# Streaming fp32 weights in five slots that hold the raw chunk and its low half in one place, instead of two raw and four split slots

## The chip, the core and the metric

The kernel runs on one core of one Trainium2 chip. Times are device microseconds of that core, for one launch. Before the change the median of three runs is 1150.75 us (1149.22 to 1153.69). A core has TensorE (PE, the matrix engine), VectorE (DVE), ScalarE (ACT), GpSimd (POOL) and SyncE (SP, which here only issues transfers), and 16 DMA engines that move data between HBM and SBUF. Each compute engine works through its own list of instructions in order and waits on semaphores for the others.

## What is computed

A trunk of two layers over 256 positions of width 1024, all in float32. Cut to what matters here:

```python
for i in range(DEPTH):                        # DEPTH = 2
    h = rmsnorm(x, norm_mix[i])
    q, k, v, cglu, sc_b, sc_c, sc_h, gates = split(h @ w_in[i])
    y_a = window_attention(q, k, v, attn_sinks[i], bias) @ w_attn_out[i]
    c = causal_dwconv(ca * sigmoid(cb), conv_dw[i]) + conv_dw_bias[i]   # 31 taps
    y_b = silu(layernorm(c, ...)) @ w_conv_out[i]
    y_c = (sc_b * causal_dwconv(sc_c * sc_h, sc_conv[i])) @ w_sc_out[i]
    mix = g[0] * y_a + g[1] * y_b + g[2] * y_c                          # g = sigmoid(gates)
    x = x + mix @ w_mix_out[i]
    h2 = rmsnorm(x, norm_ffn[i])
    x = x + (silu(h2 @ w_ffn_gate[i]) * (h2 @ w_ffn_up[i])) @ w_ffn_down[i]
    x = x + (p[i] @ w_ple[i]) * sigmoid(rmsnorm(x, norm_ple[i]) @ w_ple_gate[i])
return rmsnorm(x, norm_final)
```

Each large product is made of three: value and weight are both split into a high half (rounded to the type fp32r) and a low half (what the rounding left), and hi·hi, lo·hi and hi·lo are added in PSUM.

## The kernel before, in words

**Weights.** All weights of both layers are one stream of 184 chunks (92 a layer) of 1 MB, each 16 blocks of 128 by 128, in the order in which TensorE uses them. SP loads a chunk as it is (`w_raw`), ACT rounds it (`w_hi`, function `round_chunk`, operations on line 660), DVE subtracts (`w_lo = w_raw - w_hi`, function `low_chunk`, line 1021). `w_hi` and `w_lo` have four slots each (`RING`), `w_raw` has two (`RAW_RING`). A chunk of strips is 48 matmuls of 256 columns, one of the token-wise products (branches, FFN up and gate) 24 matmuls of 512 columns.

**What lets a chunk in.** SP's loop waits, before the load of chunk n, for `lo_ready` of chunk n-2: DVE has subtracted it and its raw slot is free (line 329, 330). ACT rounds chunk n = c + 4 in the place in its program that `after_chunk(c)` marks, and there also waits for `strip_done` to pass `AFTER[c]`, that is, until TensorE has finished chunk c = n-4, whose slot is overwritten. DVE subtracts at the same mark in its own program.

**What stands around it.** The rounding and the subtraction are placed by hand between the other work of ACT and DVE: gates, softmax, the convolution's taps on DVE (`taps`, line 1145), the products that ACT makes for POOL's convolution adds (`conv_products`, ring of four, POOL line 1476). So an engine that waits for a chunk holds up whatever its program has next. Three such places are spoken of below. In the first, `norm` of the first layer: ACT rounds chunk 2 before `root` (line 688), DVE subtracts chunk 2 before the reciprocal (line 1030) that all of `h` depends on. In the second, DVE's `branch_product` of `conv_out` (lines 1274, 1278) stands behind the subtraction of chunk 48 (140 in the second layer), and TensorE's `turn_mix` (line 546) waits for it. In the third, ACT's first FFN gate (line 948) and DVE's first FFN product (line 1365) stand behind chunk 58 (150), and TensorE's `turn_ffn` (line 582) waits for that product.

TensorE works through the chunks with `strip`, `tok_group`, `strips_late` and `strip_quad`, waits for `lo_ready` once a chunk, and adds to `strip_done` at the end of each strip. At the start SP issues x, chunk 0 in two halves, chunk 1 and the parameters (`prms`), then enters the loop. POOL transfers the relative bias: a spread of 2.5 MB at 14 us and the load of 1.5 MB of it at 58 us.

Of the kernel before, what the change touches and what calls it, by code (L numbers as in the profile page):

```python
# [25 lines left out]
P = 128  # L26
D_MODEL = 1024
SEQ = 256
DEPTH = 2
# [23 lines left out]
BPC = 16  # L53
RING = 4
RAW_RING = 2
BANKS = 4
# [13 lines left out]
STRIPS, CHUNKS = _s, _b // BPC  # L70
assert CHUNKS % RING == 0 and STRIPS % BANKS == 0
USES = STRIPS // BANKS
# [49 lines left out]
def build(nc, x, p, wstream, prm, gain, sink_rows, table, onehot, ident, out):  # L122
    ctx = ExitStack()
    with ctx:
        def sb(name, shape, dt=F32):
            return ctx.enter_context(nc.sbuf_tensor(name, shape, dt))
# [6 lines left out]

        w_raw = sb("w_raw", [P, RAW_RING, BPC * P])
        w_hi = sb("w_hi", [P, RING, BPC * P], F32R)
        w_lo = sb("w_lo", [P, RING, BPC * P], F32R)

# [72 lines left out]

        raw_loaded = [sem(f"raw_loaded{i}") for i in range(RAW_RING)]
        half_loaded = sem("half_loaded")
# [98 lines left out]
        def f32(ap):  # L311
            return ap.bitcast(F32)

        block = ctx.enter_context(nc.Block())


        @block.sync
        def _(sp):
            for k in range(2):
                sp.dma_start(xs[:, k * DT // 2:(k + 1) * DT // 2, :], x[:, k * DT // 2:(k + 1) * DT // 2, :]).then_inc(x_in[k], 16)  # L320
            half = BPC * P // 2
            sp.dma_start(w_raw[:, 0, 0:half], wstream[0][:, 0:half]).then_inc(half_loaded, 16)
            sp.dma_start(w_raw[:, 0, half:], wstream[0][:, half:]).then_inc(raw_loaded[0], 16)
            sp.dma_start(w_raw[:, 1, :], wstream[1]).then_inc(raw_loaded[1], 16)
            sp.dma_start(prms[:, :, :], prm).then_inc(prm_in, 16)

            with sp.Fori(1, DEPTH * CHUNKS // RAW_RING) as i:
                for j in range(RAW_RING):
                    sp.wait_ge(lo_ready, i * RAW_RING + j - RAW_RING + 1)
                    sp.dma_start(w_raw[:, j, :], wstream[i * RAW_RING + j]).then_inc(raw_loaded[j], 16)  # L330
            for b in range(TB):
                for h in range(2):
                    sp.wait_ge(out_dve if h else out_act, b + 1)
                    sp.dma_start(out[b, :, h * 512:(h + 1) * 512], y[:, b, h, :]).then_inc(out_stored, 16)
            sp.wait_ge(out_stored, 4 * 16)
# [3 lines left out]
        def _(pe):  # L339
            def mm3(bank, blk, hi, lo, first, last):  # L340

                slot, col = blk // BPC % RING, blk % BPC * P
                o = psum[bank][:, 0:SEQ]
                wh, wl = w_hi[:, slot, col:col + P], w_lo[:, slot, col:col + P]
                nc.tensor.matmul(o, wh, hi, start=first, stop=False, skip_group_check=True)  # L345
                nc.tensor.matmul(o, wh, lo, start=False, stop=False, skip_group_check=True)  # L346
                return nc.tensor.matmul(o, wl, hi, start=False, stop=last, skip_group_check=True)  # L347

            def strip(L, s, blk, src, ktiles, ds=0, dc=0, ready=None, amid=None, half=False):
# [5 lines left out]
                for k in range(ktiles):  # L355
                    if half and k == 0:
                        pe.wait_ge(half_low, 1)
                    elif (blk + k) % BPC == 0 or k == 0:
                        pe.wait_ge(lo_ready, L * CHUNKS + dc + (blk + k) // BPC + 1)
                    if ready is not None:  # L360
                        ready(k)
                    if amid is not None and k == AMID:
                        amid()
                    mm = mm3(bank, blk + k, hi[:, t0 + k, :], lo[:, t0 + k, :], k == 0, k == ktiles - 1)
                mm.then_inc(strip_done, 1)

            def strip_quad(L, s, blk, n):

                for k in range(DT):
                    for part in range(2):  # L370

                        pe.wait_ge(hlo_ready if part else hhi_ready, (L * 2 + n // 2) * DT + k + 1)
                        for e in range(4):
# [4 lines left out]
                            o = psum[(s + e) % BANKS][:, 0:SEQ]  # L378
                            slot, col = (blk + e * DT) // BPC % RING, (blk + e * DT + k) % BPC * P
                            wh, wl = w_hi[:, slot, col:col + P], w_lo[:, slot, col:col + P]  # L380
# [9 lines left out]
            def tok_group(L, s, c, src, bank, use, ready=None, amid=None, mid=None):  # L390

                hi, lo, t0 = src
                for half in range(2):
                    slot = (c + half) % RING
                    pe.wait_ge(lo_ready, L * CHUNKS + c + half + 1)
# [20 lines left out]
            def strips_late(L, s, blk, src, ktiles, n, early, ready, amid, amid_at):  # L416
# [3 lines left out]
                for part in (range(early), range(early, ktiles)):  # L420
                    for e in range(n):
# [5 lines left out]
                        for k in part:  # L427
# [4 lines left out]
                            if e == 0:  # L432
                                ready(k)
                            mm = mm3(bank, g, hi[:, t0 + k, :], lo[:, t0 + k, :], k == 0, k == ktiles - 1)
                        if part.stop == ktiles:
# [216 lines left out]
        def _(act):  # L652
# [8 lines left out]

            def round_chunk(L, n, after=None, dc=0, dn=0):

                act.wait_ge(raw_loaded[n % RAW_RING],
                            (L * (CHUNKS // RAW_RING) + dn // RAW_RING + n // RAW_RING + 1) * 16 if isinstance(dn, int)
                            else (L * (CHUNKS // RAW_RING) + dn + n // RAW_RING + 1) * 16)
                if after is not None:
                    act.wait_ge(strip_done, L * STRIPS + after)
                copy(w_hi[:, n % RING, :], w_raw[:, n % RAW_RING, :]).then_inc(hi_ready, 1)

# [47 lines left out]
            for L in range(DEPTH):  # L718
                def after_chunk(c, i=0):

                    if c + RING >= CHUNKS:
                        if L < DEPTH - 1:
                            round_chunk(L, c + RING, AFTER[c])
                    elif isinstance(i, int):
                        round_chunk(L, c + RING, AFTER[c])
                    else:
                        round_chunk(L, c + RING, 2 * RING * i + AFTER[c], dn=(RING // RAW_RING) * i)

# [37 lines left out]
                round_h(L * 3)  # L766
                round_chunk(L, RING - 1)
                for t in range(DT):
# [237 lines left out]
        def _(dve):  # L1006
# [8 lines left out]

            def low_chunk(L, n, after=None, dn=0):

                dve.wait_ge(hi_ready, L * CHUNKS + dn + n + 1)
                if after is not None:
                    dve.wait_ge(strip_done, L * STRIPS + after)  # L1020
                nc.vector.tensor_tensor(w_lo[:, n % RING, :], w_raw[:, n % RAW_RING, :], f32(w_hi[:, n % RING, :]),  # L1021
                                        ALU.subtract).then_inc(lo_ready, 1)
# [60 lines left out]
            for L in range(DEPTH):  # L1083
# [21 lines left out]
                raw_gate(1, 2)  # L1105
                low_chunk(L, RING - 1)
                raw_product(cv[:, 1, CPAD:], 1, 3, 1)

                def after_chunk(c, i=0):
                    if c + RING >= CHUNKS:  # L1110
                        if L < DEPTH - 1:
                            low_chunk(L, c + RING, AFTER[c])
                    elif isinstance(i, int):
                        low_chunk(L, c + RING, AFTER[c])
                    else:
                        low_chunk(L, c + RING, 2 * RING * i + AFTER[c], dn=RING * i)

# [505 lines left out]
```

## Time and profile before

| | |
|---|---|
| median of 3 runs | 1150.75 us |
| the profiled execution, its own time | 1149.08 us |
| its span, first to last instruction | 1147.3 us |
| TensorE busy | 1112.1 us (97%) |
| VectorE busy | 811.9 us (71%) |
| ScalarE busy | 697.5 us (61%) |
| GpSimd busy | 414.4 us (36%) |
| weight chunks loaded | 183 whole of 1024 KB, 2 halves of 512 KB |
| HBM read | 199.19 MB, 177 GB/s over the span |

The profile is that of one execution. A row of a timeline gives start and duration in us, engine, line, operation and, in brackets, how long the engine was idle just before and who ended that. Matmuls are pipelined: a row's duration is longer than the distance to the next one, and the distance is what the matmul costs.

### The profile page before, as it was taken

How to read it: one execution, taken by the hardware profiler on the slowest of the kernel's cores; microseconds unless marked ns; L12 is line 12 of the kernel's file. 1: busy time of each engine (PE TensorE's matmuls, PEld its weight loads, DVE VectorE, ACT ScalarE, POOL GpSimd, SP SyncE). 2: the span in 40 equal slices, each digit the busy share in tenths (PEclk: the TensorE clock that was granted, in tenths of full speed). 3: DMA queues.
4: the chain of work that ended last, by engine and by line, in shares of the span. 5: the costliest groups of instructions: out<-in, count | busy, mean ns of one | idle time of the engine just before them, and what ended most of it. 6: DMA issues, size and time to landing. Idle time of an engine off the chain costs nothing.

```text
span 1147.3 us, 19188 instructions
## 1 busy us (share of the span) xinstructions
PE 1112.1 (97%) x7190; PEld 1003.0 (87%) x7190; DVE 811.9 (71%) x1143; ACT 697.5 (61%) x1073; POOL 414.4 (36%) x405
## 2 busy tenths in 40 slices
PE   6999999999999999999999999999999999999997
PEld 5999889888798889889989988988887978998997
DVE  6887997977756554554898899888785655545555
ACT  5768987766645443444666788877574444334445
POOL 0587658783002000002228876778520200000012
PEclk9999999999999999999999999999999999999999
DMA  8565334555544554555335543345556455455441
GB/s 301 191 229 201 125 113 147 183 214 199 197 169 175 192 187 179 189 186 178 111 138 198 209 155 123 136 148 201 203 193 219 148 187 187 178 191 184 177 147 37
DMA packets 29350, 201.44 MB, mean 176 GB/s; under 512 B 3520, under 2 KB 3712, under 8 KB 5840
## 3 DMA queue, kind: packets, MB, share of 16 engines
q1 hardware_dynamic: 27648, 195.38, 47.7%
q0 software_dynamic: 1088, 4.74, 1.2%
q8 instruction: 57, 0.93, 0.3%
q14 instruction: 29, 0.24, 0.1%
q10 hardware_dynamic: 528, 0.15, 0.1%
HBM read 199.19 MB, written 3.69 MB: 177 GB/s over the span
## 4 chain that ended last, share of the span: by engine, by line
PE 49%; DVE 16%; ACT 12%; POOL 10%; DMA 7%; issue 5%; DVEq 0%; POOLq 0%; SPq 0%; ACTq 0%
POOL pacc L1476 10%; PE bank L406 8%; PE bank L408 8%; PE bank L407 8%; PE bank L345 7%; PE bank L346 7%; PE bank L347 7%; DMA w_raw<-in_wstream 6%; ACT w_hi L660 6%; DVE w_lo L1021 6%; ACT cprod L660 2%; DVE probs L1198 1%; DVE act_lo L1025 1%; PE bank L582 1%; PE bank L382 1%
## 5 line engine op out<-in xcount | busy, mean ns | idle before, releaser
L1021 DVE TENSOR_TENSOR w_lo<-w_raw,w_hi 128x2048 fp32r<-128x2048 f32 x183 | 432.2, 2365 | 228.0 <-ACT w_hi L660 215.2
L660 ACT ACTIVATE w_hi<-w_raw 128x2048 fp32r<-128x2048 f32 (+1 forms) x185 | 351.1, 1901 | 200.8 <-DMA w_raw<-in_wstream 79.7
L1476 POOL TENSOR_TENSOR pacc<-pacc,cprod 128x256 f32<-128x256 f32 x280 | 299.0, 1068 | 80.8 <-ACT cprod L660 43.5
L345 PE MATMUL bank<-h_hi,w_hi 128*128 128x256 f32 x832 | 241.8, 291 | 1.7 <-DVE w_lo L1021 0.5
L346 PE MATMUL bank<-h_lo,w_hi 128*128 128x256 f32 x832 | 236.7, 285 | 0.0
L347 PE MATMUL bank<-h_hi,w_lo 128*128 128x256 f32 x832 | 236.5, 284 | 0.0
L406 PE MATMUL bank<-w_hi,h_hi 128*128 128x512 f32 x544 | 214.6, 395 | 0.0
L408 PE MATMUL bank<-w_hi,h_lo 128*128 128x512 f32 x544 | 212.3, 390 | 0.0
L407 PE MATMUL bank<-w_lo,h_hi 128*128 128x512 f32 x544 | 212.1, 390 | 0.0
L1436 POOL TENSOR_TENSOR sqsum<-xs 128x256 f32<-128x256 f32 x6 | 3.9, 650 | 508.7 <-DVE xs L1323 458.5
L660 ACT ACTIVATE cprod<-cv,prms 128x256 f32<-128x256 f32 x310 | 141.0, 504 | 65.5 <-POOL pacc L1476 64.5
L345 PE MATMUL bank<-act_hi,w_hi 128*128 128x256 f32 x576 | 165.9, 288 | 4.5 <-DVE w_lo L1068 2.9
L345 PEld LDWEIGHTS bank<-h_hi,w_hi 128*128 128x128 f32 x832 | 160.5, 193 | 9.1 <-issue 5.4
L347 PE MATMUL bank<-act_hi,w_lo 128*128 128x256 f32 x576 | 164.3, 285 | 0.0
L346 PE MATMUL bank<-act_lo,w_hi 128*128 128x256 f32 x576 | 164.3, 285 | 0.0
L346 PEld LDWEIGHTS bank<-h_lo,w_hi 128*128 128x128 f32 x832 | 160.8, 193 | 0.0
L347 PEld LDWEIGHTS bank<-h_hi,w_lo 128*128 128x128 f32 x832 | 160.6, 193 | 0.0
L408 PEld LDWEIGHTS bank<-w_hi,h_lo 128*128 128x128 f32 x544 | 102.2, 188 | 21.7
L407 PEld LDWEIGHTS bank<-w_lo,h_hi 128*128 128x128 f32 x544 | 102.3, 188 | 20.4
L406 PEld LDWEIGHTS bank<-w_hi,h_hi 128*128 128x128 f32 x544 | 102.2, 188 | 20.3
L345 PEld LDWEIGHTS bank<-act_hi,w_hi 128*128 128x128 f32 x576 | 111.6, 194 | 6.1 <-issue 4.0
L346 PEld LDWEIGHTS bank<-act_lo,w_hi 128*128 128x128 f32 x576 | 111.7, 194 | 0.3
(174 smaller groups left out, 1442.2 us busy)
## 6 DMA issues: line engine op xcount, KB each, us to landing
w_raw<-in_wstream SPq DMA_DIRECT2D x183, 1024.0 KB, 4.9
rel_bias_rows<-rel_bias_by_distance POOLq DMA_DIRECT2D x1, 2560.0 KB, 19.4
bias<-rel_bias_rows POOLq DMA_DIRECT2D x1, 1536.0 KB, 11.3
xs<-in_x SPq DMA_DIRECT2D x2, 512.0 KB, 4.4
w_raw<-in_wstream SPq DMA_DIRECT2D x2, 512.0 KB, 7.7
out_y<-xs SPq DMA_DIRECT2D x4, 256.0 KB, 2.4
zacc<-in_p POOLq DMA_DIRECT2D x2, 256.0 KB, 3.5
prms<-in_prm SPq DMA_DIRECT2D x1, 328.0 KB, 10.3
```

Of the source, the lines that this page charges most:

```text
L345: nc.tensor.matmul(o, wh, hi, start=first, stop=False, skip_group_check=True)
L346: nc.tensor.matmul(o, wh, lo, start=False, stop=False, skip_group_check=True)
L347: return nc.tensor.matmul(o, wl, hi, start=False, stop=last, skip_group_check=True)
L382: nc.tensor.matmul(o, wh, h_hi[:, k, :], start=k == 0, stop=False, skip_group_check=True)
L406: nc.tensor.matmul(o, hi[:, t0 + kt, rows], wh, start=kt == 0, stop=False, skip_group_check=True)
L407: nc.tensor.matmul(o, hi[:, t0 + kt, rows], wl, start=False, stop=False, skip_group_check=True)
L408: mm = nc.tensor.matmul(o, lo[:, t0 + kt, rows], wh, start=False, stop=kt == DT - 1, skip_group_check=True)
L582: mm = nc.tensor.transpose(psum[6 + n % 2][:, e * SEQ + b * P:e * SEQ + (b + 1) * P], prod[:, b, e * P:(e + 1) * P], idt[:, :])
L660: return nc.scalar.activation(o, i, ACT.Identity, **kw)
L1021: nc.vector.tensor_tensor(w_lo[:, n % RING, :], w_raw[:, n % RAW_RING, :], f32(w_hi[:, n % RING, :]), ALU.subtract).then_inc(lo_ready, 1)
L1025: nc.vector.tensor_tensor(o, value, f32(hi), ALU.subtract).then_inc(sm, 1)
L1476: nc.gpsimd.tensor_tensor(o, a, cprod[:, n % PROD_RING, :], ALU.add).then_inc(pool_step, 1)
```

## The change

The raw chunk now lands where its low half will be: `w_raw` is a second name, of type float32, for the memory of `w_lo`, and the subtraction writes over its own input. The two raw slots are gone, and `w_hi` and `w_lo` have five slots, so the memory used is the same (ten slots of 8 KB in each partition). Chunk n uses slot n mod 5, counted over both layers (`slot_of`). SP's list is written out without a loop: chunks 2, 3 and 4 are issued right after the parameters with no wait, and from chunk 5 on a load waits for `strip_done`, until TensorE has finished chunk n-5. ACT's and DVE's wait on `strip_done` is gone, since the load stands behind it; ACT waits only for the load (one semaphore a slot). Where chunk n is rounded and subtracted in ACT's and DVE's programs stays (`AHEAD` = 4).

```diff
-RING = 4
-RAW_RING = 2
+RING = 5
+AHEAD = 4
...
-        w_raw = sb("w_raw", [P, RAW_RING, BPC * P])
+        low_at = -(-nc.sbuf_base // 32) * 32
+        w_lo = sb("w_lo", [P, RING, BPC * P], F32R)
+        w_raw = nc.alloc_sbuf_tensor_at("w_raw", [P, RING, BPC * P], F32, offset=low_at)
         w_hi = sb("w_hi", [P, RING, BPC * P], F32R)
-        w_lo = sb("w_lo", [P, RING, BPC * P], F32R)
...
+        def slot_of(L, n):
+
+            return (L * CHUNKS + n) % RING
+
...
-            with sp.Fori(1, DEPTH * CHUNKS // RAW_RING) as i:
-                for j in range(RAW_RING):
-                    sp.wait_ge(lo_ready, i * RAW_RING + j - RAW_RING + 1)
-                    sp.dma_start(w_raw[:, j, :], wstream[i * RAW_RING + j]).then_inc(raw_loaded[j], 16)
+            for n in range(2, DEPTH * CHUNKS):
+                if n >= RING:
+                    L, c = divmod(n - RING, CHUNKS)
+                    sp.wait_ge(strip_done, L * STRIPS + AFTER[c])
+                sp.dma_start(w_raw[:, n % RING, :], wstream[n]).then_inc(raw_loaded[n % RING], 16)
...
-            def round_chunk(L, n, after=None, dc=0, dn=0):
-
-                act.wait_ge(raw_loaded[n % RAW_RING],
-                            (L * (CHUNKS // RAW_RING) + dn // RAW_RING + n // RAW_RING + 1) * 16 if isinstance(dn, int)
-                            else (L * (CHUNKS // RAW_RING) + dn + n // RAW_RING + 1) * 16)
-                if after is not None:
-                    act.wait_ge(strip_done, L * STRIPS + after)
-                copy(w_hi[:, n % RING, :], w_raw[:, n % RAW_RING, :]).then_inc(hi_ready, 1)
+            def round_chunk(L, n):
+
+                slot = slot_of(L, n)
+                act.wait_ge(raw_loaded[slot], ((L * CHUNKS + n) // RING + 1) * 16)
+                copy(w_hi[:, slot, :], w_raw[:, slot, :]).then_inc(hi_ready, 1)
...
-            def low_chunk(L, n, after=None, dn=0):
-
-                dve.wait_ge(hi_ready, L * CHUNKS + dn + n + 1)
-                if after is not None:
-                    dve.wait_ge(strip_done, L * STRIPS + after)
-                nc.vector.tensor_tensor(w_lo[:, n % RING, :], w_raw[:, n % RAW_RING, :], f32(w_hi[:, n % RING, :]),
+            def low_chunk(L, n):
+
+                slot = slot_of(L, n)
+                dve.wait_ge(hi_ready, L * CHUNKS + n + 1)
+                nc.vector.tensor_tensor(w_lo[:, slot, :], w_raw[:, slot, :], f32(w_hi[:, slot, :]),
                                         ALU.subtract).then_inc(lo_ready, 1)
```

TensorE, DVE, ACT and POOL keep their instructions in the same order; TensorE's matmuls differ in the slot they read. What moves is SP's list. Before, from the parameters on (`lo_ready` is DVE's subtraction; the rows from the branch on are the loop):

```order
L325 DMA prms<-in_prm 128x656
L327 UNCONDITIONAL_BRANCH
L327 ISA
L330 ISA [waits lo_ready]
L330 DMA w_raw<-in_wstream 128x2048
L330 ISA [waits lo_ready]
L330 DMA w_raw<-in_wstream 128x2048
L327 REGISTER_ALU
L327 COMPARE_AND_BRANCH
```

And now (`strip_done` is TensorE's):

```order
L330 DMA prms<-in_prm 128x656
L336 DMA w_raw<-in_wstream 128x2048 x3
L336 DMA w_raw<-in_wstream 128x2048 [waits strip_done] x179
L340 DMA out_y<-xs 128x512 [waits out_act]
L340 DMA out_y<-xs 128x512 [waits out_dve]
```

Three loads have moved ahead of every wait, and the other 179 wait for TensorE instead of DVE. The second place is ACT at the start of the first layer, from the rounding of chunk 1 on. Before:

```order
L660 ACTIVATE w_hi<-w_raw 128x2048 [waits raw_loaded1]
L660 ACTIVATE w_hi<-w_raw 128x2048 [waits raw_loaded0]
L688 ACTIVATE rstd<-bank,eps 128x256 [waits ms_ready,prm_in]
L762 ACT_TABLE_LOAD
L762 ACTIVATE gated<-gated 128x256 [waits bank_read0]
L660 ACTIVATE h_hi<-hf 128x256 [waits hf_ready] x8
L660 ACTIVATE w_hi<-w_raw 128x2048 [waits raw_loaded1]
L762 ACTIVATE gated<-gated 128x256 [waits bank_read2]
L660 ACTIVATE w_hi<-w_raw 128x2048 [waits strip_done,raw_loaded0]
```

And now:

```order
L666 ACTIVATE w_hi<-w_raw 128x2048 [waits raw_loaded1]
L666 ACTIVATE w_hi<-w_raw 128x2048 [waits raw_loaded2]
L691 ACTIVATE rstd<-bank,eps 128x256 [waits ms_ready,prm_in]
L760 ACT_TABLE_LOAD
L760 ACTIVATE gated<-gated 128x256 [waits bank_read0]
L666 ACTIVATE h_hi<-hf 128x256 [waits hf_ready] x8
L666 ACTIVATE w_hi<-w_raw 128x2048 [waits raw_loaded3]
L760 ACTIVATE gated<-gated 128x256 [waits bank_read2]
L666 ACTIVATE w_hi<-w_raw 128x2048 [waits raw_loaded4]
```

The roundings stand where they stood; from chunk 4 on (the last row) they wait for a load alone, and the load of chunk 2 no longer shares a slot with chunk 0.

## Rows read from the trace of the kernel before

**Rows 1.** The page, part 1, and the view of the cores

```profile
PE 1112.1 (97%) x7190; PEld 1003.0 (87%) x7190; DVE 811.9 (71%) x1143; ACT 697.5 (61%) x1073; POOL 414.4 (36%) x405
...
core 0: 1147.3 us, clock 0.996
```

**Rows 2.** Waits of TensorE: line, releaser, us in total, times, longest us

```profile
PE bank L514 <- ACT probs_t L660: 3.8, 2, 2.2
...
PE bank L546 <- DVE qm L1278: 2.4, 4, 0.7
PE bank L490 <- DVE cv L1145: 2.0, 1, 2.0
...
PE bank L582 <- DVE prod L1365: 1.4, 2, 1.2
```

**Rows 3.** All operations on `w_raw`: idle before them by releaser; loads to landing

```profile
  DMA w_raw<-in_wstream: 79.7, 40
...
DMA to landing us min/median/max: 4.8/4.9/12.3
```

**Rows 4.** Busy time by stretch: PE, PEld, DVE, ACT, POOL (count), PEclk, DMA share, GB/s

```profile
17.40:27.80 10.40, 10.40 (x82) 10.18 (x81) 7.61 (x12) 5.60 (x8) 0.00 (x0) 1.00 1.00 349
41.60:47.30 5.70, 5.70 (x50) 5.70 (x50) 4.62 (x6) 5.43 (x10) 3.94 (x3) 1.00 0.39 129
103.30:106.50 3.20, 3.20 (x17) 3.20 (x16) 2.76 (x12) 1.13 (x3) 2.91 (x3) 0.50 0.84 302
```

**Rows 5.** Timeline of the start: SP, ACT, DVE, then TensorE at strip 4

```profile
3.45 0.45 SPq L325 DMA_DIRECT2D prms<-in_prm  x1
...
18.36 1.91 ACT L660 ACTIVATE w_hi<-w_raw 128x2048 fp32r<-128x2048 f32 x1 [3.02 <-DMA w_raw<-in_wstream]
20.18 0.46 ACT L688 ACTIVATE rstd<-bank,eps 128x256 f32<-128x256 f32 x1
...
22.52 1.75 DVE L1030 RECIPROCAL rstd<-rstd 128x256 f32<-128x256 f32 x1
...
29.06 0.39 PE L345 MATMUL bank<-h_hi,w_hi 128*128 128x256 f32 x1
...
29.79 0.39 PE L345 MATMUL bank<-h_hi,w_hi 128*128 128x256 f32 x1
```

**Rows 6.** The page, part 6: issue, KB each, median us from issue to landing

```profile
prms<-in_prm SPq DMA_DIRECT2D x1, 328.0 KB, 10.3
```

**Rows 7.** The chain of waits, 59 to 72 us; below it ACT's wait, 60 to 70 us

```profile
60.48 8.62 DMA w_raw<-in_wstream
...
ACT w_hi L660 <- DMA w_raw<-in_wstream: 1.9, 1, 1.9
```

**Rows 8.** Timeline of DVE in both layers at the last early taps, and ACT

```profile
100.69 0.86 DVE L1145 SCALAR_TENSOR_TENSOR cv<-cv,prms,bank 128x256 f32<-128x256 f32 x2
...
662.08 0.86 DVE L1145 SCALAR_TENSOR_TENSOR cv<-cv,prms,bank 128x256 f32<-128x256 f32 x2
...
667.28 1.92 ACT L660 ACTIVATE w_hi<-w_raw 128x2048 fp32r<-128x2048 f32 x1 [0.47 <-DMA w_raw<-in_wstream]
```

**Rows 9.** Timeline of ACT, DVE and TensorE at `turn_mix`, first layer

```profile
303.76 1.92 ACT L660 ACTIVATE w_hi<-w_raw 128x2048 fp32r<-128x2048 f32 x1 [2.94 <-DMA w_raw<-in_wstream]
...
305.71 2.29 DVE L1021 TENSOR_TENSOR w_lo<-w_raw,w_hi 128x2048 fp32r<-128x2048 f32 x1 [2.56 <-ACT w_hi L660]
...
309.39 0.44 PE L546 MATMUL bank<-idt,qm 128*128 128x128 f32 x2 [0.43 <-DVE qm L1278]
```

**Rows 10.** Timeline of ACT and TensorE at the first `turn_ffn`, second layer

```profile
926.44 1.92 ACT L660 ACTIVATE w_hi<-w_raw 128x2048 fp32r<-128x2048 f32 x1 [4.44 <-DMA w_raw<-in_wstream]
...
931.19 0.44 PE L582 MATMUL bank<-idt,prod 128*128 128x128 f32 x2 [1.16 <-DVE prod L1365]
```

**Rows 11.** Timeline in the FFN: chunk 64 subtracted by DVE, first matmul on it

```profile
398.22 2.29 DVE L1021 TENSOR_TENSOR w_lo<-w_raw,w_hi 128x2048 fp32r<-128x2048 f32 x1 [3.02 <-ACT w_hi L660]
...
412.55 0.39 PE L406 MATMUL bank<-w_hi,h_hi 128*128 128x512 f32 x1
```

More of the change, by code:

```diff
@@ L70 @@
 STRIPS, CHUNKS = _s, _b // BPC
-assert CHUNKS % RING == 0 and STRIPS % BANKS == 0
+assert STRIPS % BANKS == 0
 USES = STRIPS // BANKS
@@ L209, in build @@
         bias_ready = sem("bias_ready")
-        raw_loaded = [sem(f"raw_loaded{i}") for i in range(RAW_RING)]
+        raw_loaded = [sem(f"raw_loaded{i}") for i in range(RING)]
         half_loaded = sem("half_loaded")
@@ L339, in _, with mm3 @@
         def _(pe):
-            def mm3(bank, blk, hi, lo, first, last):
-                slot, col = blk // BPC % RING, blk % BPC * P
+            def mm3(L, bank, blk, hi, lo, first, last):
+                slot, col = slot_of(L, blk // BPC), blk % BPC * P
                 o = psum[bank][:, 0:SEQ]
@@ L363, in strip @@
                         amid()
-                    mm = mm3(bank, blk + k, hi[:, t0 + k, :], lo[:, t0 + k, :], k == 0, k == ktiles - 1)
+                    mm = mm3(L, bank, blk + k, hi[:, t0 + k, :], lo[:, t0 + k, :], k == 0, k == ktiles - 1)
                 mm.then_inc(strip_done, 1)
@@ L378, in strip_quad @@
                             o = psum[(s + e) % BANKS][:, 0:SEQ]
-                            slot, col = (blk + e * DT) // BPC % RING, (blk + e * DT + k) % BPC * P
+                            slot, col = slot_of(L, (blk + e * DT) // BPC), (blk + e * DT + k) % BPC * P
                             wh, wl = w_hi[:, slot, col:col + P], w_lo[:, slot, col:col + P]
@@ L393, in tok_group @@
                 for half in range(2):
-                    slot = (c + half) % RING
+                    slot = slot_of(L, c + half)
                     pe.wait_ge(lo_ready, L * CHUNKS + c + half + 1)
@@ L433, in strips_late @@
                                 ready(k)
-                            mm = mm3(bank, g, hi[:, t0 + k, :], lo[:, t0 + k, :], k == 0, k == ktiles - 1)
+                            mm = mm3(L, bank, g, hi[:, t0 + k, :], lo[:, t0 + k, :], k == 0, k == ktiles - 1)
                         if part.stop == ktiles:
@@ L718, in _, with after_chunk @@
             for L in range(DEPTH):
[L719 to L727, printed above, removed]
+                def after_chunk(c):
+                    if c + AHEAD < CHUNKS or L < DEPTH - 1:
+                        round_chunk(L, c + AHEAD)
                 def activate(u, s, func, partner, ds=0):
@@ L766, in _ @@
                 round_h(L * 3)
-                round_chunk(L, RING - 1)
+                round_chunk(L, AHEAD - 1)
                 for t in range(DT):
@@ L1105, in _, with after_chunk @@
                 raw_gate(1, 2)
-                low_chunk(L, RING - 1)
+                low_chunk(L, AHEAD - 1)
                 raw_product(cv[:, 1, CPAD:], 1, 3, 1)
[L1109 to L1116, printed above, removed]
+                def after_chunk(c):
+                    if c + AHEAD < CHUNKS or L < DEPTH - 1:
+                        low_chunk(L, c + AHEAD)
                 def gate_product(o, u, s, ds=0):
```

## The prediction

> **What bounds the kernel now.** First the busy times and the clock [rows 1]: TensorE is busy 1112.1 of 1147.3 us, 97%, so no change to the other engines can give more than its 35 us of idle time and what its clock lost. The granted clock is 0.996 on average; 0.4% of the span, 4.6 us at half rate. Then TensorE's waits [rows 2]: none of the large ones is for a weight chunk. They are for DVE and ACT: probabilities in the attention (3.8 us), the mixed branches (2.4), the convolution's taps (2.0), the FFN products (1.4). So the loads matter only where they hold DVE or ACT in front of such a result. That they do: 40 times, 79.7 us in total, ACT sat idle until a raw chunk landed [rows 3]. A load takes 4.9 us from issue to landing, at most 12.3 [rows 3], and with two raw slots it is issued when DVE has subtracted the chunk two before. Where chunks follow each other closely in ACT's program, load, rounding and subtraction form one serial loop: 4.9 + 1.9 + 2.3 = 9.1 us for two chunks, with ACT idle in between.
>
> **The change part by part.** *Removed:* that loop. A load is now issued when TensorE has finished chunk n-5. As ACT rounds chunk n in the neighbourhood of TensorE's finishing n-4, one chunk later, and a chunk lasts 48 matmuls at 0.12 us (50 in 5.70 us [rows 4]), 5.7 us, or 24 of 512 columns at twice that, 5.5 us, the 4.9 us mostly fit. I go through the places where TensorE waits behind such a load.
>
> *A, start of layer 1.* ACT waited 3.02 us for chunk 2, rounded it at 18.36 to 20.2 and only then took the root [rows 5]. DVE subtracted chunk 2 until 22.5, then the reciprocal [rows 5]. TensorE then took its tiles of h at 29.79 - 29.06 = 0.73 us each [rows 5] instead of 3 x 0.12 = 0.36: five such tiles, 1.8 us. Now chunk 2 stands behind the parameters, which land at 3.45 + 10.3 = 13.8 [rows 5, 6]. With its 1 MB at the 349 GB/s that the queues reach when full [rows 4], 3.0 us, it lands at 16.8. Rounding to 18.7, subtraction to 21.0, so the reciprocal starts at 21.0 instead of 22.5, 1.5 us earlier; the two tile rates make up the 1.8 at most, and the next wait, for chunk 3's low half, moves along. Landing at 15.5 would give all of it and some of that wait. I take 1.7, between 0.6 and 2.3.
> POOL's spread of 2.5 MB runs from about 15 us. The rows show that a load issued in it (17.9 us) needed the longest time of all, 12.3 us [rows 3], as if queued behind it, so chunk 2, queued ahead of it, should be spared. The Trainium skill ("DMA: Bandwidth & Descriptors", section on queues, rings and completion order) says instead that each DMA engine takes turns between its queues, packet by packet. By that rule chunk 2 gets half the rate from 15.3 on and lands near 18, and A gives 0.7 in place of 1.7.
>
> *B, entry of the first attention.* TensorE waited 2.0 us for DVE's taps [rows 2], which ended at 101.5 [rows 8]. Behind that wait its granted clock stood at 0.50 for 3.2 us (103.3 to 106.5 [rows 4]), 1.2 instead of 2.4 GHz, which costs 1.5 us more. The second layer has the same code without the wait (taps end at 662.9 [rows 8]). What differs is a load of 8.62 us, during POOL's bias transfer [rows 7]: ACT stood still for 1.9 of it [rows 7], and DVE's taps are 1.9 us later from there on. Now that load (chunk 10) is issued one and a half chunks earlier, since TensorE's stretch from 41.6 to 47.3 is chunk 4 [rows 4], so chunk 5 ends at 53.0, against an issue at 60.48; even 8.6 us end before ACT asks, at 69.1 - 1.9 = 67.2. The wait and the slow clock vanish: 3.4 us. POOL's own bias masking also stands in the first layer alone and may hold back 0.6 of it, and the next attention wait can take some: in the second layer it is 2.2 against 1.6 us [rows 2]. I take 2.4, between 0 and 3.5.
>
> *C, second attention.* ACT's chain to that wait of 2.2 us starts 0.47 us late on a load [rows 8]. I take 0.5; up to 1.2 if a shorter wait spares a slow clock.
>
> *D, `turn_mix`, both layers.* DVE's products stand behind the subtraction of chunk 48: load landed 303.7 after 2.94 us of ACT's waiting, subtraction 305.71 to 308.0, products, and TensorE waited [rows 9]; four waits, 2.4 us [rows 2]. A wait costs about 0.16 more than its idle time, as a matmul of 0.39 us is left to drain whose successor normally follows after 0.23: 3.0 us. When is the load due now? TensorE begins chunk 46 some 12 matmuls before the first wait (309.39 - 0.43), at 306.2, so it finished chunk 43 two chunks before, at 295.3; landed 300.2, ACT was ready at 300.8. Chunk 48 is subtracted 2.6 us earlier, more than any of these waits. I take 2.8, between 1.5 and 3.1.
>
> *E, first `turn_ffn`, both layers.* ACT waited 4.44 us for chunk 150, then loaded its table and made the gate; DVE's product came late and TensorE waited 1.16 [rows 10], 1.4 in both layers [rows 2], 1.7 with the draining. Counting back as in D from 930.03, chunk 148 began at 927.3, and with two chunks of 5.5 us and the mean square between them chunk 145 was finished by 915.0, so the load lands at 920, before ACT asks at 922.0. Then the gates wait for TensorE's strips (927.3) instead of the load, and the product is there by 929. I take 1.8 with a product half that was late too; between 1.2 and 2.1.
>
> *Added:* a load that is due later where TensorE finishes chunks in quick succession, as in the down products (4.3 or 3.6 us a chunk): 4.9 + 0.3 - 3.6 = 1.6 us later than ACT was freed before. Behind ACT's wait stand the next roundings, and behind DVE's the adds that free PSUM banks. TensorE asks for such a chunk far later: chunk 64 was subtracted at 400.5 and first used at 412.55 [rows 11]. 12 us of cover against 1.6: I cost it at nothing, at most 1 us; without the cover it would be 1.6 us for some eight chunks. The chunks at the start of each layer have the least cover (0 to 3 us), but ACT's program, not a load, set them, and it is not later now. SP's 179 waits now come from TensorE; nothing else is queued on SP but the stores at the end. The subtraction in place keeps its 2.29 us [rows 11] in my sum; the trace of before has no operation that overwrites its input at this size, so between 2.2 and 2.8.
>
> Sum: 1.7 + 2.4 + 0.5 + 2.8 + 1.8 = 9.2 us. The profiled execution took 1149.1 (span 1147.3 and 1.8 around it), so 1139.9; the median of the runs is 1.7 higher, 1150.75 - 9.2 = 1141.5.
>
> **The rivals.** *1. The waits are handed on.* Each of B to E ends in a chain of several engines, and what is late next may be almost as late: POOL's adds for the taps, the table load before the gate, the softmax. For it speaks that the second layer's attention waits longer although its taps are in time; against it that the load was the last to end in D and E, with 2.6 and 4.4 us. If A and half of D and E remain, 1.7 + 2.3 = 4.0: 1146.8; if nothing does, 1150.75. *2. Slower: the shared place.* Transfers now write into the tensor that TensorE reads and DVE overwrites. If that made a subtraction last 2.8 instead of 2.29 us, it would show where TensorE's chain passes through one: about 11 a layer in the attention and 5 at each start, 32 x 0.5 = 16 us, less the 9 gained: 1158. From about 0.3 us more on, the gain is gone. The Trainium skill ("SBUF — State Buffer", who interferes with whom) speaks against it: a DMA never contends with a compute engine there; no row tests it for one slot. *3. The loads don't start earlier in effect*, because queued transfers delay each other (12.3 us is possible) or ACT's own order is what counts: then D and E stay, and 1148 results.
>
> **How the numbers follow.** The forecast holds with 0.62 (1138.5 to 1144.5), rival 1 with 0.22 (1145 to 1151), rival 2 with 0.06, rival 3 with 0.10 (1147 to 1150). The low end is all terms at their upper bounds, 2.3 + 3.5 + 1.2 + 3.1 + 2.1 = 12.2, 1138.5, and a little for the spread of the runs: 1138. The high end takes in rival 3 and most of rival 1: 1149. What a measurement can tell from no change is 0.5%, 5.8 us, so faster means below 1145.0: 0.62 and a little of rival 1, 0.65; the same 0.29; slower 0.06.
>
> **What would show it.** The profile after should have TensorE's waits on `qm` and on the FFN product gone or below 0.3 us, no wait for the taps in the first layer and a granted clock of 1.00 around 103 us, ACT's idle time for loads far below 79.7 us and its waits for TensorE gone, and the first reciprocal at 20 to 21 us. The subtraction's duration should stay near 2.29 us. Wrong would be new waits of TensorE for `w_lo` in the down products or behind `ple_gate`, or the waits of D and E unchanged with another releaser in front of DVE.

## The result, and the profile after

The changed kernel takes 1139.4 us (median of 4 runs, 1139.2 to 1139.6) beside 1150.4 for the kernel before (4 runs, 1149.2 to 1153.7): ratio 0.990, 95% interval 0.988 to 0.992, 11 us less. The forecast was 1141.5, between 1138 and 1149. The profiled execution took 1139.2, with a span of 1137.4.

The page, part 1, of the changed kernel, and its view of the cores:

```profile
PE 1107.9 (97%) x7190; PEld 1001.0 (88%) x7190; DVE 806.9 (71%) x1143; ACT 697.3 (61%) x1073; POOL 434.5 (38%) x405
...
core 0: 1137.4 us, clock 0.997
```

Against [rows 1] every engine does the same instructions, in about the same time, but for POOL: 20 us more for the same 405. It comes back below.

TensorE's waits in the changed kernel (line, releaser: us in total, times, longest):

```profile
PE bank L464 <- DMA cprod<-in_onehot: 7.8, 1, 7.8
PE bank L520 <- ACT probs_t L666: 3.8, 2, 1.9
PE bank L509 <- DVE act_lo L1022: 3.6, 6, 1.0
PE bank L351 <- DVE w_lo L1065: 2.9, 1, 2.9
PE bank L351 <- DVE act_lo L1055: 1.6, 1, 1.6
PE bank L388 <- ACT h_hi L666: 1.6, 2, 0.8
PE bank L650 <- ACT sq L686: 0.8, 1, 0.8
PE bank L564 <- POOL sqsum L1481: 0.8, 2, 0.4
PE bank L351 <- DVE w_lo L1018: 0.6, 2, 0.3
```

The three waits of [rows 2] on which the prediction rested, for `qm` (2.4), the convolution's taps (2.0) and the FFN's `prod` (1.4), are gone. The wait for `probs_t` stayed at 3.8 in total (in the first layer it grew from 1.63 to 1.88 us, in the second it fell from 2.18 to 1.89). One is new: 0.8 us at L564, where TensorE needs the sums that POOL makes for the convolution's mean.

ACT's largest waits, of the kernel before and then of the changed one:

```profile
ACT w_hi L660 <- DMA w_raw<-in_wstream: 79.7, 40, 4.4
...
ACT w_hi L660 <- PE bank L347: 62.7, 16, 6.1
ACT w_hi L660 <- PE bank L408: 58.4, 24, 3.5
```

```profile
ACT w_hi L666 <- DMA w_raw<-in_wstream: 126.5, 53, 8.6
ACT gated L946 <- PE bank L414: 83.4, 42, 2.2
```

Roundings wait for TensorE no longer, but they wait longer for loads, 126.5 us against 79.7, and single ones far longer. The longest:

```profile
1008.96 1.91 ACT L666 ACTIVATE w_hi<-w_raw 128x2048 fp32r<-128x2048 f32 x1 [8.60 <-DMA w_raw<-in_wstream]
```

It stands in a stretch of down products, where TensorE has no wait at all. ACT is simply ahead there, and a load that was issued in time ends its idle time.

The start (time, duration, engine, operation, idle time before it) and the product in front of `turn_mix`, in the changed kernel:

```profile
16.31 1.91 ACT L666 ACTIVATE w_hi<-w_raw 128x2048 fp32r<-128x2048 f32 x1 [1.18 <-DMA w_raw<-in_wstream]
18.85 0.48 ACT L691 ACTIVATE rstd<-bank,eps 128x256 f32<-128x256 f32 x1 [0.63 <-PE bank L459]
```

```profile
20.46 1.75 DVE L1027 RECIPROCAL rstd<-rstd 128x256 f32<-128x256 f32 x1
```

```profile
295.72 1.92 ACT L666 ACTIVATE w_hi<-w_raw 128x2048 fp32r<-128x2048 f32 x1 [2.56 <-DMA w_raw<-in_wstream]
```

The rounding of chunk 2 starts at 16.31, not 18.36, and the first reciprocal at 20.46, not 22.52 [rows 5]. Chunk 48 is rounded at 295.7 instead of 303.8 [rows 9]; TensorE is 4.7 us ahead by then, so the chunk is 3.3 us earlier against it.

The entry of the first attention in the changed kernel, in the windows view (busy PE, PEld, DVE, ACT, POOL, then the granted clock, DMA share, GB/s). It is 1.00 here, and on to 106.5; [rows 4] had 0.50 from 103.3:

```profile
98.00:104.00 6.00, 6.00 (x52) 5.77 (x50) 4.55 (x13) 5.98 (x8) 4.90 (x5) 1.00 0.50 178
...
103.00:106.50 3.50, 3.50 (x32) 3.14 (x31) 3.23 (x5) 3.47 (x12) 3.21 (x3) 1.00 0.32 82
```

Where the time went, from the ends of TensorE's last matmul on each chunk in the two traces (both counted from the first instruction; after minus before, steps of a quarter us or more, in us):

```
start (chunks 0 to 2)              -2.1   (-0.4 after chunk 0 alone)
entry of the first attention       -3.3   (chunks 14 to 16)
entry of the second attention      -0.5
convolution's mean, both layers    +1.4   (+0.68, +0.67)
turn_mix, both layers              -3.3   (-1.55, -1.71)
first turn_ffn, both layers        -2.1   (-0.56, -1.51)
sum                                -9.9
```

One more thing differs between the two traces. TensorE's granted clock is 0.50 for 3.4 us at 103.3 and again at 680.1 in the kernel before, and in the changed one at 672.7 alone. TensorE is busy through these 3.4 us and does half of its work in them, so one costs 1.7 us. The stretch at 103.3 is part of the 3.3 us above.

### The profile page after: what moved, and what is told of

Its sections match the earlier page's. It is cut to its first block, busy times and chain, and to the rows that moved or that the text cites. A ratio compares the mean times of both kernels' runs of the same rounds, so it can differ in the third digit from the quotient of the medians.

```text
span 1137.4 us, 18192 instructions
## 1 busy us (share of the span) xinstructions
PE 1107.9 (97%) x7190; PEld 1001.0 (88%) x7190; DVE 806.9 (71%) x1143; ACT 697.3 (61%) x1073; POOL 434.5 (38%) x405
## 4 chain that ended last, share of the span: by engine, by line
PE 74%; DVE 11%; ACT 7%; POOL 6%; issue 2%; DMA 1%; DVEq 0%; ACTq 0%; POOLq 0%
PE bank L412 12%; PE bank L414 11%; PE bank L413 11%; PE bank L351 11%; PE bank L352 11%; PE bank L353 11%; POOL pacc L1468 4%; ACT w_hi L666 3%; DVE w_lo L1018 3%; POOL sqsum L1481 2%; ACT cprod L666 2%; DVE probs L1190 1%; PE bank L588 1%; PE bank L388 1%; PE bank L389 1%
## 5 line engine op out<-in xcount | busy, mean ns | idle before, releaser
L1018 DVE TENSOR_TENSOR w_lo<-w_raw,w_hi 128x2048 fp32r<-128x2048 f32 x183 | 427.3, 2338 | 186.1 <-ACT w_hi L666 186.1
L666 ACT ACTIVATE w_hi<-w_raw 128x2048 fp32r<-128x2048 f32 (+1 forms) x185 | 350.5, 1899 | 126.5 <-DMA w_raw<-in_wstream 126.5
```

Of the source, the lines that this page charges most:

```text
L666: return nc.scalar.activation(o, i, ACT.Identity, **kw)
L1018: nc.vector.tensor_tensor(w_lo[:, slot, :], w_raw[:, slot, :], f32(w_hi[:, slot, :]), ALU.subtract).then_inc(lo_ready, 1)
```

## The experiments

All are compared with the kernel before on the same chip; times are medians. The span of the profiled execution stands beside them where places are compared.

**All waits of the old order, in the new place.** `e0_all_waits`:

```
+                sp.wait_ge(lo_ready, n - 1)                     (each load from chunk 2 on)
...
+                if n >= AHEAD:                                  (in round_chunk; in low_chunk with dve)
+                    act.wait_ge(strip_done, L * STRIPS + AFTER[n - AHEAD])
```

> The changed kernel with all waits of the old order put back: load n also waits for the subtraction of chunk n-2, and ACT's rounding and DVE's subtraction of chunk n wait for TensorE's finishing chunk n-4. In place and five slots stay. If the gain is all in when things may start, this gives the time of the kernel before, 1149 to 1151 us. If the place itself (subtraction in place, five slots) brings or costs something, it lands that much beside: under 1146 would mean that the place itself gains.

Measured: 1148.2 us, ratio 0.998 (0.997 to 0.999); span 1146.6. The place as such, subtraction in place and five slots, costs nothing; it brings 0.7 us by the spans and 2 by the ratio (1 to 4). When things may start is the rest.

**The old issue rule alone**, that is the first of these three lines. `e1_old_issue`:

> Only the old issue rule put back on the changed kernel: load n also waits for the subtraction of chunk n-2; ACT and DVE don't wait for TensorE. Theory 1, my prediction's (the load that is issued late is what holds ACT and DVE): most of the gain goes, 1146 to 1150 us. Theory 2 (the waits of ACT and DVE for TensorE were part of the loop; without them two chunks in 9.1 us outrun TensorE's two in 11.4, so the loads run ahead by themselves): 1140 to 1144 us.

Measured: 1147.8 us, ratio 0.998 (0.997 to 1.000); span 1145.4.

**The mirror image**, the other lines without the first. `e6_tensor_waits`:

> The mirror image: loads as in the changed kernel (after TensorE's chunk n-5), but rounding and subtraction of chunk n wait for TensorE's finishing n-4, as before. Theory 1: 1139.5 to 1142 us, as the loads have landed by then (4.9 us against a chunk of 5.7). Theory 2: 1145 to 1150 us.

Measured: 1138.5 us (1138.0 to 1138.7), ratio 0.990 (0.989 to 0.992); span 1136.6. The pair decides for theory 1. Waiting for TensorE before a rounding costs nothing if the load is there. Issuing the load late costs nearly all, even though ACT and DVE may then run ahead as they like: that freedom is worth 1.2 us between the first two spans, nothing between their ratios (0.998 both), and nothing between the mirror image and the changed kernel. TensorE's waits with the old issue rule alone:

```profile
PE bank L521 <- ACT probs_t L667: 4.4, 2, 2.2
...
PE bank L497 <- DVE cv L1138: 1.7, 1, 1.7
PE bank L553 <- DVE qm L1271: 1.6, 3, 0.7
```

and ACT's in the mirror image:

```profile
ACT w_hi L666 <- PE bank L414: 81.9, 32, 3.5
...
ACT w_hi L666 <- PE bank L353: 47.6, 10, 6.2
ACT w_hi L666 <- DMA w_raw<-in_wstream: 28.1, 11, 3.1
```

The second group also settles what ACT's idle time for loads means: 171.8 us in the slow kernel with the old rule, 126.5 in the changed one, 28.1 in this equally fast one. It is no measure of lateness.

**Single terms.** The old issue rule for some loads only, by a condition such as `if n in (2, 3, 4):` in front of the first line. Term A, `e2_old_start`, chunks 2 to 4:

> The changed kernel with the old issue rule for chunks 2, 3 and 4 alone. My term A (1.7 us predicted, 1.6 read from the traces): 1141.0 to 1141.5 us, the first reciprocal back at about 22.5 us. If the early landing of chunk 2 comes from elsewhere, or the next wait takes the gain: 1139.4, no change.

Measured: 1141.1 us, span 1139.1, 1.7 more than the changed kernel's. The reciprocal is back:

```profile
22.39 1.75 DVE L1029 RECIPROCAL rstd<-rstd 128x256 f32<-128x256 f32 x1
```

Term B, `e5_old_bias`, chunks 5 to 16:

> The changed kernel with the old issue rule for chunks 5 to 16 alone, the loads around POOL's bias transfer. Term B (3.4 us predicted at most, 3.3 read from the traces): 1142 to 1143.5 us, TensorE's wait for DVE's taps back at about 101 us and a granted clock of 0.50 behind it. If the stall of the kernel before had another cause than the loads (POOL's own masking): 1139.4 to 1140.

Measured: 1142.4 us (ratio 0.993, 0.991 to 0.994), span 1141.3, 3.9 more. ACT waits 1.74 us for a load at 67.2, and TensorE waits for the taps again:

```profile
67.24 1.92 ACT L668 ACTIVATE w_hi<-w_raw 128x2048 fp32r<-128x2048 f32 x1 [1.74 <-DMA w_raw<-in_wstream]
```

```profile
99.74 0.50 PE L498 MATMUL bank<-kk,qm 64*128 64x128 f32 x4 [1.79 <-DVE cv L1139]
```

The windows view of the same kernel, with the granted clock behind POOL's figures:

```profile
99.00:108.00 9.00, 8.26 (x70) 7.68 (x71) 5.98 (x15) 6.37 (x8) 7.51 (x8) 1.00 0.42 137
```

The clock is 1.00, where the kernel before had 0.50 after the same wait [rows 4]. So the loads bring the tap wait back, but not the slow clock. Even so TensorE loses 3.1 us at chunks 14 to 16, where the changed kernel had gained 3.3: 1.85 with the tap wait and 1.26 in the next two chunks. There it idles 0.17 and 0.35 us for DVE's probabilities, and 2.19 instead of 1.88 for `probs_t`. The kernel before has no wait for probabilities there and only 1.63 for `probs_t`; with every load late and the clock at 1.00 (`e0_all_waits`, `e1_old_issue`) it is 2.2. So the matmuls at half rate seem to have given DVE and ACT time to catch up, which is argued and not tested.

Nor does the clock go by the loads alone. In the next two runs, which have the old rule on loads from chunk 44 on only, it fell in the first attention, ahead of everything that they change (windows view of `e10_old_run`; in `e3_old_mix_ffn` it is 115.1 to 118.5), and not in the second, where the changed kernel has its stretch:

```profile
114.30:117.70 3.40, 3.40 (x22) 2.73 (x17) 3.33 (x6) 2.64 (x8) 3.11 (x3) 0.50 0.46 190
```

In front of it stands the same wait for `probs_t` as in the changed kernel (1.86 us, 1.88 there). So a wait of the same length is followed by the slow clock in one place in one execution and in the other place in the next, and what decides it stays open.

Terms D and E, `e3_old_mix_ffn`, four loads of 182:

> The changed kernel with the old issue rule for four loads of 182 alone, those of chunk 48 and chunk 58 of each layer (140 and 150 in the second, counted through). Terms D and E (3.3 and 2.1 read from the traces): 1144.8 us if these loads by themselves hold the products in front of turn_mix and turn_ffn; the waits of TensorE on qm and prod return, 2.4 and 1.4 us. If the loads before them carry the delay (the rule makes a loop over many chunks), a single late load costs little, since the subtraction two before is by now early: 1139.5 to 1141.

Measured: 1142.5 us (1141.7 to 1144.2), ratio 0.993 (0.992 to 0.995); the profiled execution is the fastest of the four, its span 1139.7, 2.3 more. TensorE's list has

```profile
PE bank L590 <- DVE prod L1359: 1.6, 2, 1.3
```

again, and nothing on `qm`. By place the loss is 0.65 and 1.65 us at the two `turn_ffn` (2.07 had been gained) and nothing at `turn_mix`. One load a layer explains the whole of E. It doesn't explain D: with the old rule chunk 48 is issued at 292.1 instead of 290.7, since subtraction 46 is early by now.

So I took the five loads in front of it, `e10_old_run`:

> The changed kernel with the old issue rule for a run of five loads in each layer, chunks 44 to 48 (136 to 140). Chunk 48 alone under the old rule cost nothing at turn_mix. If term D comes from the loop over several chunks, which starts where DVE is late with subtraction 44 behind the convolution's normalisation: the waits on qm return (about 2.4 us in four) and 1142.7 us. If it comes from still earlier loads or from ACT's and DVE's waits for TensorE: 1139.4 to 1140.5.

Measured: 1139.5 us, span 1137.7: no change again, and no wait on `qm`. The rounding of chunk 48 comes 1.3 us later than in the changed kernel, less than the slack that it has:

```profile
292.10 1.92 ACT L668 ACTIVATE w_hi<-w_raw 128x2048 fp32r<-128x2048 f32 x1 [0.49 <-DMA w_raw<-in_wstream]
297.00 1.92 ACT L668 ACTIVATE w_hi<-w_raw 128x2048 fp32r<-128x2048 f32 x1 [2.98 <-DMA w_raw<-in_wstream]
```

With the rule on every load `turn_mix` lost 1.43 and 1.18 us. D is the issue rule's, then, but as a delay that is handed on from load to load over more than five chunks. Counted against TensorE's end of chunk 38, that chunk's subtraction already begins 2.2 us later in the kernel before (252.0 with 267.7) than in the changed one (245.1 with 263.0), six chunks ahead of the run that I put back. How much of it the five loads carry can be read from the start of subtraction 48 (140), counted back from TensorE's end of chunk 45 (137), the chunk before the one in which `turn_mix` stands: it comes 3.9 and 4.0 us before that end in the changed kernel, 2.7 and 1.8 with the rule on five loads, 0.7 and 0.9 with the rule on every load, 0.5 and 0.4 in the kernel before. The five loads take 1.2 and 2.3 us of this lead, and TensorE waits only when the rest is gone too. In which earlier load that rest begins was not tried.

**The price of the slot.** `e7_four_slots`: `RING = 5` becomes `RING = 4`.

> The changed kernel with four slots instead of five, so that load n waits for TensorE's chunk n-4, and rounding and subtraction stay where they stand in the programs. Each load is about 5.7 us later than in the changed kernel. Theory 1: ACT waits 4.9 us for nearly every chunk again, and at each of turn_mix, turn_ffn and the attention's entry the chunk comes about as late as before or later: 1148 to 1160 us. If a lead of one chunk is enough cover for DVE and ACT almost everywhere: 1140 to 1145.

Measured: 1234.1 us, ratio 1.074 (1.072 to 1.077), far worse than I allowed. TensorE's list starts

```profile
PE bank L588 <- DVE prod L1357: 26.2, 18, 1.7
PE bank L520 <- ACT probs_t L666: 13.8, 10, 2.6
PE bank L552 <- DVE qm L1270: 11.7, 8, 2.5
```

and ACT waits for loads 116 times, 382.5 us. The load is now issued when ACT wants to round the chunk, so ACT stands still before 116 of its 185 roundings, 3.3 us on average, and TensorE waits for 18 of the FFN's products; by the ends of its chunks it loses about 1.8 us at each of them. Part of the loss is clock: TensorE is busy for 35.5 us at 0.50 here and for 3.4 in the changed kernel, which costs some 16 of the 93 us (an estimate, half of the difference).

`e11_four_slots_lead3`: in addition `AHEAD = 3`, without the roundings and subtractions of chunk 2 ahead of the loop.

> The changed kernel with four slots, and rounding and subtraction one chunk later in the programs (three ahead of TensorE instead of four). A load then has again one chunk of TensorE's time, 5.7 us, between its issue and ACT's rounding, as with five slots. If it is this distance that decides: 1139 to 1143 us, TensorE's waits as with five slots and perhaps some for w_lo where a chunk is used soon after (layer starts, up to 3 us). If it is the lead of the low half over TensorE, or the number of slots as such: over 1150.

Measured: 1183.7 us, ratio 1.028 (1.026 to 1.031); span 1183.3. A miss as a time, but the places tell what was right:

```profile
PE bank L388 <- DVE w_lo L1017: 16.9, 2, 8.4
PE bank L351 <- issue: 16.5, 3, 6.4
...
PE bank L351 <- DVE w_lo L1017: 3.4, 2, 2.5
PE bank L412 <- DVE w_lo L1017: 3.0, 2, 1.5
```

("issue" means that the view names no releaser.) In the attention, the branches and the FFN it keeps pace with five slots to within 2 us a layer. Nearly all of the 46 us is lost at `ple_gate` (L388, four strips that start two chunks at once) and at the layer starts: 7.7 at the first, 25 around the second, 11 at the last `ple_gate`. These places also have the slow clock, 22.5 us of busy TensorE at 0.50 against 3.4, so some 10 of the 46 us are clock (estimated in the same way) and the rest is waiting. One chunk's time between issue and rounding is what ACT and DVE need; three chunks of lead are too few where chunks are used in pairs. Five slots with four ahead give both.

**The new wait.** `e8_mean_late`:

```
-                pe.wait_ge(csum_step, L * 2 * (DT - 1) + DT - 1)
-                nc.tensor.matmul(psum[4][:, 0:SEQ], ones[:, :], sqsum[:, :], ...).then_inc(cmean_done, 1)
+                def mean():                                     (the same two lines)
...
-                branch("sc_out", sc_src, js=range(2, 4), mid=variance)
+                branch("sc_out", sc_src, js=range(2, 4), amid=mean, mid=variance)
```

ACT's copy of the mean moves behind the gates.

> The changed kernel with TensorE's matmul for the convolution's mean set one third of a group of strips later (after the first token tile of the third group of sc_out), and ACT's copy of the mean behind the gates. In the changed kernel TensorE waits there 0.4 us in each layer for POOL's sums, of which five of seven are stretched by DVE's subtractions. If this wait is the whole of the 0.68 and 0.67 us that the changed kernel lost there: the wait is gone and 1138.0 to 1138.6 us. If the mean is needed at once by DVE and the later chain (variance, convolution) is tight: a new wait at the variance or the mixing, 1139.4 or more.

Measured: 1139.9 us, span 1138.2. The wait at the mean is gone and TensorE gains 0.67 us there in each layer. Three chunks on it loses 0.96:

```profile
PE bank L569 <- POOL sqsum L1489: 1.3, 2, 0.7
```

the same releaser, now at the variance. The chain POOL, mean, DVE, ACT, POOL, variance has no slack to give. In the mirror image of above (waits for TensorE kept) the wait at the mean does not occur, which is 0.5 to 0.6 us a layer and all of its lead over the changed kernel by the traces.

**Versions meant to beat both.** `e9_half_first`: the mirror image, and ACT's copy of `rel_bias` moved behind the rounding of chunk 0's first half, as the expectation says.

> A version meant to beat both: loads as in the changed kernel, the waits of ACT and DVE for TensorE kept (1138.5 us by the run with them), and in addition ACT rounds the first half of chunk 0 before it copies TensorE's first small product to SBUF (rel_bias). ACT's first rounding starts at 8.5 instead of 9.5 us, and TensorE's first strip follows it: 1137.5 us. If the half chunk has not landed by 8.5 us, no change: 1138.5.

Measured: 1138.3 us (1138.2 to 1138.7), ratio 0.989 (0.988 to 0.991). TensorE's first wait for a low half falls from 2.9 to 2.5 us only, as the half chunk lands at 8.95:

```profile
8.95 1.06 ACT L666 ACTIVATE w_hi<-w_raw 128x1024 fp32r<-128x1024 f32 x1 [0.42 <-DMA w_raw<-in_wstream]
```

`e12_probs_first`: in addition, in the attention,

```
+                    if j == 1:
+                        copy_probs(0)
                     if j < QT:
                         exponentials(j)
-                    if 0 <= j - 1 < QT:
+                    if 1 <= j - 1 < QT:
                         copy_probs(j - 1)
```

> A version meant to beat both: the kernel with kept waits and the first half chunk ahead (1138.3 us), and ACT copies the first head pair's transposed probabilities before the second pair's exponentials, not after them. TensorE's wait for probs_t, 1.9 us in each layer, should fall to about 0.3; the second pair's exponentials come 0.85 us later. 1135 us if no later wait grows; 1137 if the softmax's next steps take half of it; 1138.3 if the wait only moves to the next pair.

Measured: 1139.2 us (1139.0 to 1140.0), nothing gained. The wait for `probs_t` fell to 0.2, and this took its place: in TensorE's waits, in its timeline, and behind it in the windows view.

```profile
PE bank L509 <- DVE act_lo L1028: 7.6, 7, 2.6
```

```profile
120.36 0.84 PE L509 MATMUL bank<-idt,probs 128*128 128x128 f32 x6 [2.57 <-DVE act_lo L1028]
```

```profile
121.50:123.80 2.30, 2.30 (x12) 2.30 (x12) 2.23 (x5) 2.30 (x8) 0.73 (x1) 0.50 0.03 7
```

Without the swap that wait is 0.85. The next pair's softmax sets the time. Behind the longer wait TensorE's granted clock was 0.50, 1.2 instead of 2.4 GHz, through the 2.3 us shown and 3.4 in all, from 121.3 on. That doesn't explain the missing gain, as the version without the swap has a stretch of the same length, at 672.6, where this one has none. The best measured is thus the mirror image with or without the half chunk ahead, 1138.3 to 1138.5, about 1 us below the changed kernel, which was timed in another series, so that this microsecond rests on the spans (1136.4 and 1136.6 against 1137.4) and on the ranges of the runs, which don't overlap.

## Why the prediction was right, and where it wasn't

The mechanism holds. DVE and ACT stood behind loads that were issued late; issue them a chunk earlier and the waits go. The issue rule alone takes the gain back, and the removal of ACT's and DVE's waits for TensorE contributes next to nothing.

*A*, 1.7 forecast: 2.1 in the traces at the end of chunk 2, 1.7 by the experiment. Chunk 0 ends 0.4 earlier in the changed kernel's trace, but that is not a gain beside A. In the eight traces above in which loads 2 to 4 follow the new rule and the ring has five slots, chunk 0 ends anywhere from 20.6 to 22.0 us and chunk 2 at 33.3 to 33.6; in the four with the old rule it is 21.0 to 22.4 and 35.0 to 35.3. The landing, for which the prediction gave 16.8 with the queues served in order, was 16.3 by the rounding's start. The prediction drew 18 from the Trainium skill ("DMA: Bandwidth & Descriptors", section on queues, rings and completion order), by which each DMA engine takes turns between its queues. The landing came earlier, but it doesn't refute the rule: POOL's spread was issued at 15.97 us and its first packet moved at 19.1, so chunk 2 had nothing to take turns with, and both versions of the working had the spread flowing too early.

*B*, 2.4 with 3.5 as the upper end: 3.3. I had kept 1 us back for POOL's masking and for the next attention wait. The attention's wait took 0.25 of it (1.63 to 1.88 us), the masking nothing that shows. The term was under-sized by that deduction. The loads of chunks 5 to 16 account for 3.1 of the 3.3, but not in the way that the prediction added it up, 2.0 of wait and 1.5 of slow clock: in the experiment it is 1.85 at the tap wait and 1.26 in the two chunks behind it, with the clock at 1.00. That the slow clock followed from this wait was argued and doesn't hold there, and that both sums come out alike is luck.

*C*, 0.5: 0.5 in the traces, 0.3 of it the shorter wait for `probs_t`. No run tests it.

*D*, 2.8 with 3.1 as the upper end: 3.3. The size was nearly right, the step was not. The prediction read the load of chunk 48 as the cause because its landing ended the wait. Putting the old rule back on it, or on five loads, cost nothing. Its arithmetic for the new issue time does hold (TensorE done with chunk 43 at 290.67, load issued at 290.69); what it missed is that the old lateness had built up over many loads.

*E*, 1.8: 2.1, at its upper end, and caused by the one load named.

*Added costs, at nothing*: no wait for `w_lo` came up in the down products or behind `ple_gate`, and the subtraction took 2.28 to 2.85 us with 2.29 in the middle, as before, so rival 2 falls. What the sum left out is the convolution's mean, +1.4 us: it asked who waits for DVE and ACT, but not whose work overlaps with them once they are early. POOL's sums, as a line of the view of `sqsum`, before and after (count, then ns min/median/max):

```profile
L1489 POOL TENSOR_TENSOR sqsum<-sqsum,cv x12: 633/738/2657, 250.8 to 817.3; 128x256 f32<-128x256 f32 x12
```

```profile
L1481 POOL TENSOR_TENSOR sqsum<-sqsum,cv x12: 635/1922/2666, 245.8 to 814.0; 128x256 f32<-128x256 f32 x12
```

The sum of the terms was 9.2, the parts that it names gave 11.3, the missed one took 1.4, and 9.9 remained in the traces. So the forecast was near in part because terms that were too small and a cost that was left out worked against each other. Rival 1 came true in that small part. Rival 3 did not: loads were issued a chunk earlier in effect.

One signature was wrong. ACT's idle time for loads was to fall far below 79.7 us and rose to 126.5. ACT no longer waits for TensorE and so meets the load first. All its waits before roundings together, for loads and for TensorE, fell from 201 to 126.5.

## What to carry to other kernels

When a load is released by the step that consumed the slot's contents two chunks earlier, the load, the conversion and the next release form a loop; tie the load to the final consumer, a full chunk's time ahead of the conversion, and give the slot for it. Test such a cause by putting the old condition back on single loads, since the load that ends a wait need not be the one that caused it. Idle time "for a load" on an engine that runs ahead says nothing about the end of the program: look at TensorE's waits.

## What the runs showed of the hardware

DVE and POOL hold each other up. In the changed kernel an add of POOL on 128x256 takes 0.64 to 0.74 us alone and 2.57 to 2.67 when it starts while DVE is at a chunk's subtraction, about the subtraction's own length:

```profile
242.38 2.85 DVE L1018 TENSOR_TENSOR w_lo<-w_raw,w_hi 128x2048 fp32r<-128x2048 f32 x1
...
243.16 2.57 POOL L1481 TENSOR_TENSOR sqsum<-cv 128x256 f32<-128x256 f32 x1
245.81 10.97 POOL L1481 TENSOR_TENSOR sqsum<-sqsum,cv 128x256 f32<-128x256 f32 x6
```

The subtraction takes 2.85 there instead of 2.29. An add that was already running when a subtraction began (at 251.98 us, the subtraction at 252.43) took its usual 0.73. The same six adds took 6.58 us in the kernel before, where only one of them started beside a subtraction. Whether memory or issue is shared, no run here tells apart.

A load that is issued into POOL's bulk transfer starts late, and then shares the engines with it. POOL issues a spread of 2.5 MB at 16.0 us in the changed kernel. Its first packet moves at 19.1, when the loads queued before are nearly done. Chunk 5 is issued at 21.65; from 21.0 to 25.3 us only the spread's packets move (the queues in the DMA view of 21 to 25.3 us; q0 is POOL's, q1 is SP's; packets, MB, share of 16 engines):

```profile
q0 software_dynamic: 317, 1.62, 103.6%
```

The load's first packet moves at 25.38, 3.7 us after its issue, where a load with nothing else under way takes 0.96. From then on packets of both move side by side (25.4 to 32 us):

```profile
q1 hardware_dynamic: 214, 1.63, 70.8%
q0 software_dynamic: 102, 0.45, 26.0%
```

The load landed at 32.62, after 11.0 us instead of 4.9. In the kernel before, chunk 3 was issued at 17.85, its first packet moved at 21.8, and it landed after 12.3. Why the first packet comes so late, no run here shows. The late landing took nothing from the end, as ACT asked for chunk 5 at 35.
